# Banded convolution of a Conformer layer in eight time phases, its bands loaded from DRAM

## The chip, the cores and the metric

The kernel runs on one core of a Trainium2 chip. TensorE (PE) multiplies, VectorE (DVE), ScalarE (ACT) and GpSimd (POOL) work on elements, SyncE (SP) issues most of the DMAs; the engines run their own streams of instructions and meet only at semaphores. The metric is the device time of one launch in microseconds, lower is better.

## The reference

A decoder trunk of two layers on 512 tokens of 1024 channels, in float32: a Conformer convolution layer, then an attention layer, each followed by a mixture of experts. The change touches only the convolution of the first:

```python
def conformer_conv(h, w_in, b_in, w_dw, b_dw, ln_g, ln_b, w_out, b_out):
    u = h @ w_in + b_in
    a, gate = jnp.split(u, 2, axis=-1)
    u = a * jax.nn.sigmoid(gate)
    u = lax.conv_general_dilated(
        u, w_dw[:, None, :], window_strides=(1,), padding=[(CONV_KERNEL - 1, 0)],
        dimension_numbers=("NWC", "WIO", "NWC"), feature_group_count=D_MODEL) + b_dw
    u = jax.nn.silu(layer_norm(u, ln_g, ln_b))
    return u @ w_out + b_out
```

The convolution is depthwise and causal with 31 taps: each channel has its own filter over time.

## The kernel before

The 1024 channels are eight tiles of 128 partitions, with 512 time steps along the row. For each tile c the layer does this.

- `project_in(c)` on TensorE: 48 matmuls of 512 columns into two PSUM banks. A float32 operand is split into a leading part (`wih`, made by ScalarE's `leading_in`) and a trailing part (`wil`, VectorE's `trailing_in`), and three products are added. TensorE waits for `trailing_in(c)`, and for `gated(c - 2)`, which frees the banks.
- `sigmoid(c)` on ScalarE, `gated(c)` on VectorE: the gated product. ScalarE's stream is `leading_in(c)`, `sigmoid(c - 1)`, `leading_in(c + 1)` and so on; `leading_in(c)` waits until projection c - 2 is done.
- The convolution. Tiles 0, 2 and 4 (`BY_TAPS`) go over VectorE, 31 instructions each (`taps(c, first, last)`, then `tapped(c)`). Tiles 1, 3, 5, 6, 7 (`BY_BANDS`) go over TensorE in `convolve(c)`, with n = 0 to 4 as their place in that list.

For TensorE, time is cut in `PH` phases and the channels in `PH` blocks of `CB = 128 / PH`. The partitions then hold (phase, channel of one block), and for each block q a sum of `LAGS` matmuls with banded 128 x 128 weights `band[n % 2][:, q, m, :]` runs over `TP = 512 / PH` columns. A float32 matmul shows in the trace as two records. The tile gets into this form through DRAM: SP's `into_phases(c)` writes it to `u_dram` after `gated(c)`, waits, and reads it back in `PH` copies; `convolve(c)` waits for them. After it VectorE's `biased(c)` adds the bias into `yph`, and SP's `out_of_phases(c)` writes this to `c_dram`, waits, and reads it back into `HTQ` in `PH` copies.

The bands are built on VectorE by `spread(c)`: one product of 4608 elements per partition, of the taps with a diagonal of ones.

The mean over all channels (for the layer norm) is a matmul with 1/1024: VectorE adds up tiles 0 to 5 in `lnstd`, TensorE takes that sum, then tile 6 from `HTQ`, which waits for its way back from DRAM, and tile 7 straight from `yph[0]` in `PH` x `PH` matmuls with `onesp`. VectorE then subtracts the mean (`ln_d`), ScalarE squares, TensorE sums the squares, and the output projection follows.

Every engine's order is that of the code. SP's is one list of waits and copies: a step at its head that has to wait holds all that stand behind it. PE's order is projections 0, 1, 2, convolution 1, projections 3, 4, convolution 3, projections 5, 6, convolution 5, projection 7, convolutions 6 and 7.

Of the kernel before, what the change touches and what calls it, by code (L numbers as in the profile page):

```python
# [37 lines left out]
P = 128  # L38
D = 1024
# [19 lines left out]
PH = 4  # L59
CB = P // PH  # L60
TP = T // PH
# [26 lines left out]
C_BIN, C_BDW, C_LNG, C_LNB, C_ONE, C_TAP, C_WDW = 0, 16, 48, 56, 64, 96, 192  # L88
CONV_COLS = C_WDW + len(BY_BANDS) * PH * LAGS * PH

# [53 lines left out]
def build_program(nc, a):  # L144
# [7 lines left out]
    with ExitStack() as ctx:  # L152
# [95 lines left out]
        b_out_sb = cut(WR, 3 * 4096, D)  # L248
        WE = cut(WR, 52 * 256, 2, D)
# [4 lines left out]
        band = [at(f"band{b}", 108 + 18 * b, [P, PH, LAGS, P]) for b in range(2)]  # L254
# [18 lines left out]
        lnsq = [cut(SC, o + b * T, T) for b in range(2)]  # L273
        o += 2 * T
        onesf = cut(SC, o, P)
        o += P
        onesp = cut(SC, o, PH, P)
        o += PH * P
# [3 lines left out]
        o += T  # L282
        assert o <= 7680 - KT * (EG + E)
# [127 lines left out]
        wol_done, presum_done, band_set = [], [], []  # L411
# [83 lines left out]
        spread_set = Later(ln_n, KT + 1)  # L495
        spread_mm, spread_sb = Later(var_mm, KT), Later(sig_done, KT)
# [29 lines left out]
        def _(sp):  # L526
# [44 lines left out]
            into_phases(3)  # L571
            out_of_phases(1)
            win_load(7)
# [140 lines left out]
        def _(pool):  # L714
# [8 lines left out]
            nc.gpsimd.memset(onesp, 0.0).then_inc(conv_init, 1)  # L723
            pool.wait_ge(conv_init, 5)
            for r in range(PH):
                nc.gpsimd.memset(onesp[r * CB:(r + 1) * CB, r, :], 1.0 / D).then_inc(conv_init, 1)
                pool.wait_ge(conv_init, 6 + r)
# [113 lines left out]
        def _(act):  # L841
            act.dma_start(ident[:, :], a["ident"]).then_inc(const_in, 16)
            act.dma_start(vn[:, :], a["norm_vecs"]).then_inc(const_in, 16)
            act.dma_start(c16[:, :], a["c16"]).then_inc(const_in, 16)
            def norm_act(k):
# [48 lines left out]
            act.dma_start(b_out_sb[0:2 * CB, :], a["b_out"].to_broadcast([2 * CB, D])).then_inc(bout_in, 16)  # L894
# [27 lines left out]
            for h in range(2):  # L922
                nc.scalar.activation(bo[0:2 * CB, h * 512:(h + 1) * 512], b_out_sb[0:2 * CB, h * 512:(h + 1) * 512], ACT.Copy).then_inc(bout_added, 1)
            act.wait_ge(conv_init, 5 + PH)
            act.wait_ge(ug_out, 16 * len(BY_BANDS))
            nc.scalar.activation(bones[0:2 * CB, :], onesf[0:2 * CB, :], ACT.Copy, scale=float(D // CB)).then_inc(bout_added, 1)
# [265 lines left out]
        def _(dve):  # L1192
# [50 lines left out]
            def spread(c):  # L1243


                i, n = BY_BANDS.index(c), PH * LAGS * PH
                if i >= 2:
                    dve.wait_ge(conv_mm, i - 1)
                steps.mark(V.tensor_tensor(
                    band[i % 2][:, :, :, :].rearrange("p q m (r c) -> p (q m r) c", r=PH),  # L1250
                    cv[:, C_ONE:C_ONE + CB].rearrange("p (o c) -> p o c", o=1).to_broadcast([P, n, CB]),
                    cv[:, C_WDW + i * n:C_WDW + (i + 1) * n].rearrange("p (n o) -> p n o", o=1).to_broadcast([P, n, CB]),
                    ALU.mult))
                band_set.append(steps.n)

# [40 lines left out]
            spread(1)  # L1296
# [10 lines left out]
            spread(3)  # L1307
            taps(2, 0, 6)
            gated(3)
            biased(1)  # L1310
# [18 lines left out]
            spread(7)  # L1329
            taps(4, 14, 22)  # L1330
            gated(7)
# [1101 lines left out]
```

## Time and profile before

| | us |
|---|---|
| median of 3 runs | 1481.43 |
| lowest, highest | 1480.38, 1485.12 |
| the profiled execution, its time | 1482.62 |
| its span, first to last instruction | 1480.8 |
| the convolution layer's projections and convolutions in it | 16.5 to 146.1 |

The page of the profile gives busy times over the span; the timeline and the views by stretch show single stages; the chain of waits goes back from the last instruction, at each step to what released it. Rows of these views stand below in numbered groups.

### The profile page before, as it was taken

The numbers are of one execution on the slowest core, as the hardware profiler recorded it, in microseconds if no ns is written. First come the engines' busy times: TensorE is split into PE (matmuls) and PEld (weight loads), VectorE is DVE, ScalarE is ACT, GpSimd is POOL, SyncE is SP. The second block draws the span as 40 slices with busy tenths as digits, with TensorE's granted clock in tenths as the row PEclk, the third lists the DMA queues.
The fourth block names the chain that finished last, engine by engine and source line by source line (L and its number), as shares of the span: only waits on it lengthen the run. The fifth ranks groups of instructions, "written<-read, shape, count | busy, mean of one in ns | idle before, by whom it ended". The sixth has DMA issues, their size and how long they took to land.

```text
span 1480.8 us, 20665 instructions
## 1 busy us (share of the span) xinstructions
PE 1420.7 (96%) x7296; PEld 1156.7 (78%) x7296; DVE 1128.1 (76%) x1647; ACT 785.9 (53%) x1024; POOL 457.8 (31%) x330
## 2 busy tenths in 40 slices
PE   7999997999999997999999999999998899999997
PEld 5889685788888865888888888888887588888863
DVE  6999728888888869766858667585753888888866
ACT  5211835777777736344252533424353677777733
POOL 0000014344444410422405133150402544444310
PEclk9999997999999999999999999999999999999999
DMA  5242516899999954222212122131546599999872
GB/s 218 86 135 90 213 54 258 324 373 380 383 385 393 373 220 179 91 71 71 85 57 99 57 85 71 57 99 57 197 142 239 203 357 378 383 386 376 324 316 107
DMA packets 52765, 309.87 MB, mean 209 GB/s; under 512 B 10544, under 2 KB 16432, under 8 KB 38896
## 3 DMA queue, kind: packets, MB, share of 16 engines
q1 hardware_dynamic: 42128, 291.48, 51.3%
q0 software_dynamic: 9792, 16.80, 3.1%
q10 hardware_dynamic: 800, 1.00, 0.2%
q8 instruction: 27, 0.44, 0.1%
q14 instruction: 18, 0.15, 0.0%
HBM read 299.27 MB, written 28.84 MB: 222 GB/s over the span
## 4 chain that ended last, share of the span: by engine, by line
PE 87%; DVE 6%; DMA 2%; ACT 2%; issue 2%; POOL 0%; SPq 0%; DVEq 0%; POOLq 0%; ACTq 0%
PE PS L2185 5%; PE PS L2186 5%; PE PS L2187 5%; PE PS L2039 4%; PE PS L2038 4%; PE PS L2042 4%; PE PS L2025 4%; PE PS L2026 4%; PE PS L2027 4%; PE PS L2074 3%; PE PS L2075 3%; PE PS L2078 3%; PE PS L2201 3%; PE PS L2203 3%; PE PS L2202 3%; PE PS L2063 2%
## 5 line engine op out<-in xcount | busy, mean ns | idle before, releaser
L832 POOL TENSOR_TENSOR KQ<-rope_ab 64x512 f32<-64x512 f32 x96 | 173.6, 1809 | 316.5 <-DVE rope_ab L1698 312.9
L1573 DVE TENSOR_TENSOR wgl<-WR,wgh 128x2048 fp32r<-128x2048 f32 x66 | 150.9, 2293 | 39.3 <-ACT wgh L999 39.3
L1110 ACT ACTIVATE wh<-wraw 128x1024 fp32r<-128x1024 f32 x76 | 80.3, 1058 | 174.3 <-PE PS L2187 170.0
L1573 DVE TENSOR_TENSOR wul<-WR,wuh 128x2048 fp32r<-128x2048 f32 x66 | 148.4, 2288 | 5.2 <-issue 5.2
L1620 DVE TENSOR_TENSOR wdl<-WR,wdh 128x2048 fp32r<-128x2048 f32 x56 | 128.2, 2289 | 25.8 <-ACT wdh L1032 25.8
L1698 DVE TENSOR_TENSOR rope_ab<-PS,rope_sb 32x512 f32<-32x512 f32 x192 | 131.9, 687 | 2.6
L999 ACT ACTIVATE wuh<-WR 128x2048 fp32r<-128x2048 f32 x66 | 122.8, 1908 | 10.9 <-PE PS L2027 10.9
L1032 ACT ACTIVATE wdh<-WR 128x2048 fp32r<-128x2048 f32 x56 | 107.4, 1919 | 36.6 <-PE PS L2078 36.6
L999 ACT ACTIVATE wgh<-WR 128x2048 fp32r<-128x2048 f32 x66 | 125.1, 1903 | 0.0
L1680 DVE TENSOR_TENSOR wl<-wraw,wh 128x1024 fp32r<-128x1024 f32 x76 | 94.6, 1245 | 31.6 <-ACT wh L1110 30.1
L2038 PE MATMUL PS<-wgh,xgh 128*128 128x512 f32 x264 | 108.7, 412 | 1.4 <-ACT xgh L1015 1.4
L2039 PE MATMUL PS<-wgl,xgh 128*128 128x512 f32 x264 | 105.0, 398 | 0.0
L2025 PE MATMUL PS<-wuh,xgh 128*128 128x512 f32 x264 | 103.0, 390 | 0.0
L2027 PE MATMUL PS<-wuh,xgl 128*128 128x512 f32 x264 | 102.7, 389 | 0.0
L2026 PE MATMUL PS<-wul,xgh 128*128 128x512 f32 x264 | 102.7, 389 | 0.0
L769 POOL TENSOR_TENSOR idle<-ident_sb 128x1 f32<-128x1 f32 x30 | 20.8, 695 | 261.1 <-ACT SC L1053 248.9
L2074 PE MATMUL PS<-wdh,hTh 128*128 128x512 f32 x224 | 91.1, 407 | 0.0
L2075 PE MATMUL PS<-wdh,hTl 128*128 128x512 f32 x224 | 88.2, 394 | 0.0
L770 POOL DMA_INDIRECT y_dram<-SC,HTQ x30 | 79.4, 2646 | 5.3 <-issue 5.3
L2201 PE MATMUL PS<-HTh,wh 128*128 128x512 f32 x192 | 77.1, 402 | 0.0
L2203 PE MATMUL PS<-HTh,wl 128*128 128x512 f32 x192 | 74.9, 390 | 0.0
L2202 PE MATMUL PS<-HTl,wh 128*128 128x512 f32 x192 | 74.9, 390 | 0.0
(371 smaller groups left out, 3519.9 us busy)
## 6 DMA issues: line engine op xcount, KB each, us to landing
WR<-w_gate SPq DMA_DIRECT2D x33, 2048.0 KB, 12.0
WR<-w_up SPq DMA_DIRECT2D x33, 2048.0 KB, 9.3
WR<-w_down SPq DMA_DIRECT2D x33, 2048.0 KB, 12.0
wraw<-w_qkv SPq DMA_DIRECT2D x72, 512.0 KB, 3.3
WR<-w_in SPq DMA_DIRECT2D x8, 1024.0 KB, 4.9
xn_dram<-SC SPq DMA_DIRECT2D x8, 512.0 KB, 2.8
SC<-y_dram SPq DMA_DIRECT2D x8, 512.0 KB, 6.0
HT<-y_dram SPq DMA_DIRECT2D x8, 512.0 KB, 9.2
```

The lines of the kernel that those rows point to most:

```text
L832: nc.gpsimd.tensor_tensor(to, cos, sin, ALU.add).then_inc(rope_done, 1)
L999: nc.scalar.activation(dst[:, kts, :], src[:, kts, :], ACT.Copy).then_inc(done, 1)
L1573: V.tensor_tensor(lo[:, kts, :], raw[:, kts, :], hi[:, kts, :].bitcast(F32), ALU.subtract).then_inc(done, 1)
L1620: V.tensor_tensor(wdl[b][:, :, cols], wd[b][:, :, cols], wdh[:, :, :].bitcast(F32), ALU.subtract).then_inc(dl_done[l].sem, 1)
L1698: ins = V.tensor_tensor(rope_ab[d:d + 32, 2 * (t % 2) + 1, :], src[s:s + 32, :], rope_t[s:s + 32, tab + 1, :], ALU.mult)
L2025: M.matmul(dst, xgh[b][:, kt, :], hi[:, kt, :], start=kt == 0, stop=False)
L2026: M.matmul(dst, xgh[b][:, kt, :], lo[:, kt, :], start=False, stop=False)
L2027: ins = M.matmul(dst, xgl[b][:, kt, :], hi[:, kt, :], start=False, stop=kt == KT - 1)
L2038: M.matmul(PS[0][:, :], xgh[b][:, kt, :], wgh[:, kt, :], start=kt == 0, stop=False)
L2039: M.matmul(PS[0][:, :], xgh[b][:, kt, :], wgl[b][:, kt, :], start=False, stop=False)
L2074: M.matmul(to, hTh[:, ft, :], wdh[:, ft, :], start=ft == 0, stop=False)
L2075: M.matmul(to, hTl[:, ft, :], wdh[:, ft, :], start=False, stop=False)
```

## The change

`PH` becomes 8, so `CB` is 16, `TP` 64 and `LAGS` 5: a tile's convolution is 8 x 5 matmuls of 64 columns in place of 4 x 9 of 128, and each way into or out of phases reads back in 8 copies of 32 KB in place of 4 of 64 KB. The bands are laid out on the host, 20 KB per partition and tile, and ScalarE's queue loads them (`band_load`); `spread` and its constants are gone. The phases of tile 7 are summed by one VectorE reduction, so the mean takes 8 matmuls of 64 columns for them in place of 16 of 128. `b_out` is repeated over 32 rows as before, now named `BR`; `onesp` is one broadcast copy on GpSimd.

```diff
-PH = 4
+PH = 8
 CB = P // PH
+BR = 32
...
-        band = [at(f"band{b}", 108 + 18 * b, [P, PH, LAGS, P]) for b in range(2)]
+        band = [at(f"band{b}", 104 + 20 * b, [P, PH, LAGS, P]) for b in range(2)]
...
+        band_in = [Later(const_in, 48), Later(cvec_in, 16)]
...
             into_phases(3)
+            win_load(7)
             out_of_phases(1)
-            win_load(7)
             sp.dma_start(WE, a["w_out"][:, 0:2, :]).then_inc(wout_in[0], 16)
             out_of_phases(3)
...
+            def band_load(n):
+
+                if n >= 2:
+                    act.wait_ge(conv_mm, n - 1)
+                act.dma_start(band[n % 2].rearrange("p q m c -> p (q m c)"), a["bands"][n]).then_inc(band_in[n % 2].sem, 16)
...
             leading_in(1)
+            band_load(0)
             sigmoid(0)
             for c in range(2, KT):
                 leading_in(c)
                 sigmoid(c - 1)
+                if c % 2 == 0:
+                    band_load(c // 2)
+            band_load(4)
             sigmoid(KT - 1)
...
             trailing_in(4)
-            spread(3)
             taps(2, 0, 6)
             gated(3)
-            biased(1)
             taps(2, 6, 9)
...
             gated(4)
+            biased(1)
+            gated(5)
+            trailing_in(7)
             biased(3)
-            taps(4, 0, 3)
-            gated(5)
-            spread(5)
-            taps(4, 3, 4)
-            trailing_in(7)
-            spread(6)
-            taps(4, 4, 6)
+            taps(4, 0, 8)
             gated(6)
-            taps(4, 6, 14)
+            taps(4, 8, 14)
             biased(5)
-            spread(7)
-            taps(4, 14, 22)
+            taps(4, 14, 27)
             gated(7)
-            taps(4, 22, CONV)
+            taps(4, 27, CONV)
...
             biased(7)
+            dve.wait_ge(yph_done, len(BY_BANDS))
+            steps.mark(V.tensor_reduce(phase_sum, yph[0].rearrange("p (q t) -> p t q", q=PH), AX, ALU.add))
+            phases_summed.append(steps.n)
...
-                pe.wait_ge(v_steps, band_set[n])
+                pe.wait_ge(band_in[n % 2].sem, band_in[n % 2].at(16 * (n // 2 + 1)))
...
-            pe.wait_ge(yph_done, len(BY_BANDS))
+            pe.wait_ge(v_steps, phases_summed[0])
             for r in range(PH):
-                for q in range(PH):
-                    ins = M.matmul(PS[4][:, r * TP:(r + 1) * TP], onesp[:, r, :], yph[0][:, q * TP:(q + 1) * TP],
-                                   start=False, stop=r == PH - 1 and q == PH - 1)
+                ins = M.matmul(PS[4][:, r * TP:(r + 1) * TP], onesp[:, r, :], phase_sum, start=False, stop=r == PH - 1)
```

How the order moves is seen at two places. The first is VectorE between the last step of tile 2's taps and `gated(6)`; L1265 is `gated`, L1290 `biased`, L1249 `spread`, `wil` is written by `trailing_in`, L1273 to L1278 are taps. Before:

```order
L1282 TENSOR_TENSOR HTQ<-taps_sb 128x512 [waits v_steps]
L1265 SCALAR_TENSOR_TENSOR taps_sb<-PS,SC 128x4x128 [waits sig_done,taps_done]
L1290 TENSOR_TENSOR SC<-PS,SC 128x512 [waits conv_mm]
L1273 TENSOR_SCALAR taps_sb<-taps_sb,SC 128x512 [waits glu_done]
L1275 TENSOR_SCALAR taps_sb<-taps_sb,SC 128x512
L1278 SCALAR_TENSOR_TENSOR taps_sb<-taps_sb,SC 128x512 [waits v_steps]
L1265 SCALAR_TENSOR_TENSOR SC<-PS,SC 128x512 [waits ug_out,sig_done]
L1249 TENSOR_TENSOR band_115<-SC 128x4608 [waits conv_mm]
L1278 SCALAR_TENSOR_TENSOR taps_sb<-taps_sb,SC 128x512 [waits v_steps]
L1237 TENSOR_TENSOR wil_122<-WR,wih_120 128x2048 [waits lead_done]
```

And now, with `trailing_in` at L1250:

```order
L1282 TENSOR_TENSOR HTQ<-taps_sb 128x512 [waits v_steps]
L1265 SCALAR_TENSOR_TENSOR taps_sb<-PS,SC 128x8x64 [waits sig_done,taps_done]
L1290 TENSOR_TENSOR SC<-PS,SC 128x512 [waits conv_mm]
L1265 SCALAR_TENSOR_TENSOR SC<-PS,SC 128x512 [waits ug_out,sig_done]
L1250 TENSOR_TENSOR wil_122<-WR,wih_120 128x2048 [waits lead_done]
L1290 TENSOR_TENSOR SC<-PS,SC 128x512 [waits conv_mm]
L1273 TENSOR_SCALAR taps_sb<-taps_sb,SC 128x512 [waits glu_done]
L1275 TENSOR_SCALAR taps_sb<-taps_sb,SC 128x512
L1278 SCALAR_TENSOR_TENSOR taps_sb<-taps_sb,SC 128x512 [waits v_steps] x6
L1265 SCALAR_TENSOR_TENSOR SC<-PS,SC 128x512 [waits ug_out,sig_done]
```

The first L1290 of the old rows is `biased(3)`, right behind `gated(4)`; in the new rows the first is `biased(1)`, and `biased(3)` is the second, behind `gated(5)` and `trailing_in(7)`.

The second place is SP's queue from the way into phases of tile 3 to that of tile 5. Before (L546, L553 into phases, L559, L563 out of them, L540 a load of `w_in`, L574 and L576 loads of `w_out`):

```order
L559 DMA c_dram<-SC 128x512 [waits yph_done]
L563 DMA HTQ<-c_dram 32x4x128 [waits yph_out]
L563 DMA HTQ<-c_dram 32x4x128 x3
L540 DMA WR<-w_in 128x2048 [waits wil_done]
L574 DMA WR<-w_out 128x2x1024
L559 DMA c_dram<-SC 128x512 [waits yph_done]
L563 DMA HTQ<-c_dram 32x4x128 [waits yph_out]
L563 DMA HTQ<-c_dram 32x4x128 x3
L576 DMA WO<-w_out 128x2x1024
L546 DMA u_dram<-SC 128x512 [waits glu_done]
L553 DMA SC<-u_dram 32x4x128 [waits conv_mm,conv_init,ug_out]
L553 DMA SC<-u_dram 32x4x128 x3
```

And now:

```order
L546 DMA WR<-w_in 128x2048 [waits wil_done]
L565 DMA c_dram<-SC 128x512 [waits yph_done]
L569 DMA HTQ<-c_dram 16x8x64 [waits yph_out]
L569 DMA HTQ<-c_dram 16x8x64 x7
L580 DMA WR<-w_out 128x2x1024
L565 DMA c_dram<-SC 128x512 [waits yph_done]
L569 DMA HTQ<-c_dram 16x8x64 [waits yph_out]
L569 DMA HTQ<-c_dram 16x8x64 x7
L582 DMA WO<-w_out 128x2x1024
L552 DMA u_dram<-SC 128x512 [waits glu_done]
L559 DMA SC<-u_dram 16x8x64 [waits conv_mm,conv_init,ug_out]
L559 DMA SC<-u_dram 16x8x64 x7
```

The load of `w_in` for projection 7 moved ahead of tile 1's way out; the ways out of tiles 1 and 3 still stand ahead of the way in of tile 5, each with twice the copies.

## Rows read from the trace of the kernel before

**Rows 1.** The page, busy time of each engine over the span.

```profile
PE 1420.7 (96%) x7296; PEld 1156.7 (78%) x7296; DVE 1128.1 (76%) x1647; ACT 785.9 (53%) x1024; POOL 457.8 (31%) x330
```

**Rows 2.** TensorE by stretch: us, busy (records), granted clock, DMA share, GB/s.

```profile
99.10:110.00 10.90, 10.90 (x49) 1.00 0.53 164
110.00:118.90 8.90, 8.20 (x74) 1.00 0.13 44
```

**Rows 3.** Chain of waits, 93 to 120 us: start, us, what.

```profile
96.53 2.94 DMA c_dram<-SC
...
101.29 0.43 SPq L576
...
101.77 5.68 DMA u_dram<-SC
...
108.76 1.97 DMA SC<-u_dram
...
110.78 8.30 PE PS L1946 x72
```

**Rows 4.** Chain of waits, 0 to 260 us, TensorE's runs of records.

```profile
130.01 16.08 PE PS L1946 x144
146.09 0.86 PE PS L1967 x2
...
147.81 3.58 PE PS L1973 x32
...
205.31 1.70 PE PS L1835 x16
```

**Rows 5.** Groups by line and shape, 0 to 240 us: busy us, mean ns.

```profile
L1249 DVE TENSOR_TENSOR band<-SC 128x4608 f32<-128x4608 f32 x5 | 24.8, 4951 | 0.0
...
L1835 PE MATMUL PS<-SC,XT 128*128 128x20 f32 x64 | 8.4, 277 | 0.8 <-DVE XT L1384 0.8
```

**Rows 6.** The page, DMA issues: count, KB each, median us to landing.

```profile
WR<-w_up SPq DMA_DIRECT2D x33, 2048.0 KB, 9.3
...
WR<-w_in SPq DMA_DIRECT2D x8, 1024.0 KB, 4.9
```

**Rows 7.** DMA issues, 0 to 200 us: count, KB each, median us to landing.

```profile
u_dram<-SC SPq DMA_DIRECT2D x5, 256.0 KB, 2.0
SC<-u_dram SPq DMA_DIRECT2D x20, 64.0 KB, 2.0
```

**Rows 8.** Timeline of SP's queue, 0 to 165 us: start, us of issuing, copies.

```profile
43.13 1.75 SPq L553 DMA_DIRECT2D SC<-u_dram  x4
...
72.93 1.76 SPq L553 DMA_DIRECT2D SC<-u_dram  x4
...
135.84 0.43 SPq L582 DMA_DIRECT2D WO<-w_out  x1
139.87 0.34 SPq L559 DMA_DIRECT2D c_dram<-SC  x1
142.78 1.74 SPq L563 DMA_DIRECT2D HTQ<-c_dram  x4
```

**Rows 9.** Timeline, 95 to 111 us, VectorE and ScalarE: start, us, instruction.

```profile
95.83 0.67 DVE L1290 TENSOR_TENSOR SC<-PS,SC 128x512 f32<-128x512 f32 x1
...
99.23 0.69 ACT L903 ACTIVATE SC<-PS,SC 128x512 f32<-128x512 f32 x1 [16.45 <-PE PS L1935]
...
99.82 1.91 ACT L891 ACTIVATE wih<-WR 128x2048 fp32r<-128x2048 f32 x1
...
106.15 2.29 DVE L1237 TENSOR_TENSOR wil<-WR,wih 128x2048 fp32r<-128x2048 f32 x1
```

**Rows 10.** TensorE by stretch around an idle time, columns as in the second group.

```profile
164.70:167.40 2.70, 2.67 (x6) 0.50 1.10 464
167.80:170.50 2.70, 2.70 (x14) 1.00 0.74 309
```

**Rows 11.** VectorE's groups by line and shape: a reduction.

```profile
L1538 DVE TENSOR_REDUCE HTQ<-HTQ 128x8 f32<-128x384 f32 x2 | 1.1, 555 | 0.1
```

More of the change, by code:

```diff
@@ L87 @@
                  ((0, 0, 0), (0, 1, 0), (0, 1, 1), (0, 2, 0)), ((0, 2, 1), (0, 3, 0), (0, 3, 1)))
-C_BIN, C_BDW, C_LNG, C_LNB, C_ONE, C_TAP, C_WDW = 0, 16, 48, 56, 64, 96, 192
-CONV_COLS = C_WDW + len(BY_BANDS) * PH * LAGS * PH
+C_BIN, C_BDW, C_LNG, C_LNB, C_SEL, C_TAP = 0, 16, 80, 88, 96, 104
+CONV_COLS = C_TAP + len(BY_TAPS) * (CONV + 1)
 class Steps:
@@ L273, in build_program @@
         lnsq = [cut(SC, o + b * T, T) for b in range(2)]
+        onesp = cut(SC, o, PH, P)
+        assert PH * P <= 2 * T
         o += 2 * T
@@ L276, in build_program @@
         o += P
-        onesp = cut(SC, o, PH, P)
-        o += PH * P
+        b_out_sb = cut(SC, o, D)
+        o += D
         cv = cut(SC, o, CONV_COLS)
@@ L282, in build_program @@
         o += T
+        phase_sum = cut(SC, o, TP)
+        o += TP
         assert o <= 7680 - KT * (EG + E)
@@ L410, in build_program @@
         fin_g = cut(WR, 4096, D)
-        wol_done, presum_done, band_set = [], [], []
+        wol_done, presum_done, phases_summed = [], [], []
         beats = {(l, stage): [] for l in range(2) for stage in ("rank", "rows")}
@@ L722, in _ @@
                 nc.gpsimd.memset(uph[b][:, :, 0:LAGS - 1], 0.0).then_inc(conv_init, 1)
[L723 to L727, printed above, removed]
+            pool.wait_ge(cvec_in, 16)
+            nc.gpsimd.tensor_copy(onesp, cv[:, C_SEL:C_SEL + PH].rearrange("p (r o) -> p r o", o=1).to_broadcast([P, PH, P])).then_inc(conv_init, 1)
             def moe_pool(l):
@@ L922, in _ @@
             for h in range(2):
[L923 to L924 removed]
+                nc.scalar.activation(bo[0:2 * BR, h * 512:(h + 1) * 512], b_out_sb[0:2 * BR, h * 512:(h + 1) * 512], ACT.Copy).then_inc(bout_added, 1)
+            act.wait_ge(conv_init, 4)
             act.wait_ge(ug_out, 16 * len(BY_BANDS))
[L926 removed]
+            nc.scalar.activation(bones[0:2 * BR, :], onesf[0:2 * BR, :], ACT.Copy, scale=float(D // BR)).then_inc(bout_added, 1)
             act.wait_ge(conv_mm, len(BY_BANDS))
@@ L1242, in _ @@
             dve.wait_ge(cvec_in, 16)
[L1243 to L1254, printed above, removed]
             def gated(c):
@@ L1844, in project_out @@
                         for h in range(2):
-                            M.matmul(PS[2 * n + h][:, :], bones[0:2 * CB, :], bo[0:2 * CB, h * 512:(h + 1) * 512], start=True, stop=False)
+                            M.matmul(PS[2 * n + h][:, :], bones[0:2 * BR, :], bo[0:2 * BR, h * 512:(h + 1) * 512], start=True, stop=False)
                     for n in range(NT):
@@ L1962, in _ @@
             convolve(7)
-            pe.wait_ge(conv_init, 4)
-            pe.wait_ge(conv_init, 9)
+            pe.wait_ge(conv_init, 5)
             pe.wait_ge(v_steps, presum_done[0])
@@ L2397, in lay_out @@
     by_block = np.tile(f["a_b_dw"][0].reshape(KT * PH, CB).T, (PH, 1))
-    same = np.tile(np.eye(CB, dtype=np.float32), (PH, 1))
+    of_phase = (np.arange(P)[:, None] // CB == np.arange(PH)).astype(np.float32) / np.float32(D)
+    taps_of = np.zeros((len(BY_BANDS), PH, CB, PH, LAGS, PH, CB), np.float32)
+    for c in range(CB):
+        taps_of[:, :, c, :, :, :, c] = bands[:, c][:, list(BY_BANDS)].transpose(1, 0, 2, 3, 4)
     a = {"x": f["x"]}
@@ L2402, in lay_out @@
     a["ffn_norm"] = f["ffn_norm"].reshape(2, 1, D)
-    a["conv_vecs"] = asc(cat([by_tile(f["a_b_in"][0]), by_block, by_tile(f["a_ln_g"][0]), by_tile(f["a_ln_b"][0]), same, taps,
-                              bands[:, :, list(BY_BANDS)].reshape(P, -1)], 1))
+    a["conv_vecs"] = asc(cat([by_tile(f["a_b_in"][0]), by_block, by_tile(f["a_ln_g"][0]), by_tile(f["a_ln_b"][0]), of_phase, taps], 1))
+    a["bands"] = taps_of.reshape(len(BY_BANDS), P, PH * LAGS * P)
     a["w_in"] = asc(f["a_w_in"][0].reshape(P, KT, 2, KT, P).transpose(3, 0, 1, 2, 4).reshape(KT, P, KT * 2 * P))
```

8 lines of the change are left out of this document (3 added, 5 removed).

## The prediction

> **What bounds the kernel now.** The page comes first: TensorE (PE) is busy 96% of the span [rows 1]. Next come the busy times by stretch: over the projections and convolutions of layer 0 TensorE is full, and the one gap is 0.7 us before the convolution of tile 5 [rows 2]. The reader is to see that there VectorE's work, long as it is, already hides under TensorE. Third, the chain of waits up to that gap shows what the slack hangs on [rows 3]: VectorE's `biased(3)` ends at 96.5, SP writes tile 3 to `c_dram` (2.94 us), issues its reads, one 1 MB load of `w_out`, then the write of tile 5 to `u_dram` (5.68 us, since the megabyte is ahead of it in the same queue), then the reads of tile 5, and `convolve(5)` starts at 110.78. From the end of `biased(3)` to that matmul are 14.25 us, and they fit only because `biased(3)` comes 2.6 us before TensorE ends projection 5 (about 99.1).
>
> **The change part by part.** All numbers are on the clock of the trace of before until the sum.
>
> *Convolution on TensorE.* A tile was 4 x 9 matmuls of 128 columns and is now 8 x 5 of 64. A matmul in float32 shows as two records, so 72 records become 80. Now 144 records take 16.08 us, 111.7 ns each [rows 4]. Do 64 columns cost half? The router's matmuls stream 20 columns against weights of 128 columns, also float32 [rows 5], and 16 of them take 1.70 us, 106.3 ns each [rows 4]. With a sixth of the columns the record is hardly shorter: the weight load sets it. So 64 columns cost between 106.3 and 111.7 ns; I take 106.3, as the fewer columns lie below the load. 80 x 106.3 ns = 8.50 us against 8.04, so +0.46 a tile, +2.3 us for five (4.5 at the upper price). All of it is on the path, as TensorE is full. The Trainium skill (TensorE: Matmul & The Clock Gate, section LDWEIGHTS) says that a weight load costs by its columns, P / 1.2 ns, 107 ns for 128, whatever streams afterwards; it speaks against the halving, and by it the five tiles come to +2.6 us, while by the same page's section Back-to-back issue gap, whose isolated gap counts the moving columns alone, they would shrink; the 20-column row agrees with the first.
>
> *Bands from DRAM.* Five VectorE instructions, 24.8 us in all, go [rows 5]. They hide under TensorE today, so this gives nothing by itself: `gated(1)`, `gated(3)`, `gated(5)` and `trailing_in(6)` wait for ScalarE's steps, which wait for TensorE. Instead ScalarE issues five loads of 2.5 MB. 1 MB lands in 4.9 us and 2 MB in 9.3 [rows 6]; 2.5 MB in some 9 to 12. Every band is asked for 10 us or more before its convolution (the last right after `convolve(5)`, 19 us before `convolve(7)`), so no band is late. But bands 1 and 2 are issued just as SP sends tiles 1 and 3 through DRAM. See below.
>
> *Small copies.* Each way back from DRAM is eight issues instead of four, some 0.48 us apart (four take 1.75 us, each lands 2.0 after its issue) [rows 7, 8], so the last piece is 1.9 us later. Before, tile 1's four reads were issued from 43.13 on and had landed at about 46.6, for a convolution at 50.3: slack 3.7. With 1.9 more it is 1.8. Tile 3 has its reads from 72.93 and the convolution at 80.1: slack 3.7, then 1.8. The band load beside each takes some of it; the write and the reads may each be a microsecond or two slower. I take 0.5 us of wait at each, +1.0 together (0 to 10, see the second rival). Pieces are 256 B instead of 512 B. The Trainium skill (DMA: Bandwidth & Descriptors, Specifications) puts the least size for full rate at 512 B, which no row here tests; at 32 KB a copy I leave the term as it is.
>
> *The reordering, the main term.* `biased(3)` stood right after `gated(4)`. Now `biased(1)`, `gated(5)` and `trailing_in(7)` are ahead of it, and both of these wait for the end of projection 5. ScalarE: the sigmoid starts at 99.23, the next step at 99.82 [rows 9]. Between them now lies one DMA issue, say 0.45, so the leading part runs 100.3 to 102.2, `trailing_in(7)` takes 2.25 and `biased(3)` 0.6 [rows 9]: it ends at about 105.0 instead of 96.5. SP's order has not followed: `out_of_phases(3)` is still ahead of `into_phases(5)`. The chain of 14.25 us starts at 105.0 and is longer by two sets of four issues, 3.8 us: 18.1, ending at 123.1. There is more ahead of its first write: `out_of_phases(1)` is now late too (`biased(1)` ends about 96.5, eight reads until 102.5), so the 1 MB load WE goes out at about 103 rather than 79.8, and band load 3 (2.5 MB, issued about 100) is in flight; a write behind 1 MB took 5.68 [rows 3] against a median of 2.0 [rows 7]. I take +2 (0 to 4.5): `convolve(5)` can start at 125.1, and TensorE is ready at 109.9. It waits 15.2 us instead of 0.9, +14.3. If the write of tile 5 were not held by the megabyte ahead of it (2.0 for 5.68) and the first write not at all, +8.6; at the other end +16.8. Queued behind the wait are projection 7 and convolutions 6 and 7; VectorE stands at `biased(5)` and ScalarE at band load 4 meanwhile.
>
> *Clock.* After the idle stretch up to 164.7 TensorE has a granted clock of 0.50, the 1.2 GHz level, for 2.7 us and 1.00 after it [rows 10]. A wait of 15 us should end so as well: some 3.4 us at half pace, +1.7 (0 to 2).
>
> *Tile 7.* `gated(7)` ends about 1.9 us after projection 7; write 2.0, last issue 3.4, landing 2.0: 9.3 us after the projection's end, while convolution 6 takes 8.5. +0.8 (0 to 2).
>
> *The mean.* 32 records of 3.58 us [rows 4] become 16, 1.7 us at 106.3: -1.9. VectorE's reduction reads 512 elements (384 took 0.56 [rows 11]), 0.6 to 1.1 us, and lies with `biased(7)` beside the two matmuls of 1.72 us before it. Given back: the second of these waits for tile 6 from DRAM. Its write sits behind the load of `w_out` that TensorE's last projection releases; one such write took from 139.87 to 142.78 with that load 4 us ahead [rows 8], now it is 1.6 ahead, and eight issues follow. That lands 10.1 us after `convolve(6)`, against 9.4 for `convolve(7)` and the first matmul: +0.7. Net -1.2. The late `w_out` load of `out_of_phases(7)` arrives about when ScalarE wants it.
>
> **Sum.** 2.3 + 1.0 + 14.3 + 1.7 + 0.8 - 1.2 = 18.9. Later stages follow in the same order, shifted. The profiled execution took 1482.6 with a span of 1480.8; 1482.6 + 18.9 = 1501.5. It lay 1.2 above the median of the three runs, so between 1500.3 and 1501.5: I say 1501.
>
> **Rivals.** *A, the forecast:* `convolve(5)` starved through `biased(3)`, 1501.
>
> *B, the small copies are held at every band load.* If the write and reads of tiles 1 and 3 get through only once the band is in (9 to 12 us after its issue at 40.3 and 70.1, then 5.4 for reads), those convolutions wait 4.5 to 7 us each: 1501.5 - 1.0 + 9 to 14 = 1510 to 1515. For: the 5.68 us write. Against: that one stood behind a load in its own queue, and the bands come from another. The Trainium skill (DMA: Bandwidth & Descriptors, Queues, rings and completion order) has each DMA engine go round its queues by packets, which would keep the small copies moving; no row here shows two queues at once.
>
> *C, not slower: the columns set the price.* Two records of 512 columns take 0.86 us [rows 4], 0.84 ns a column; 64 would be 54 ns and a tile 4.3 us, 3.7 less than before. Five tiles: -18.7 in place of +2.3; tile 7 then waits about 5.0 instead of 0.8; the mean saves 0.8 more: 1501.5 - 21.0 + 4.2 - 0.8 = 1484, no change, and with the short end of the wait (5.7 less) 1478, faster. It decides from a record of some 60 ns on. Against: the 20-column row at 106 ns.
>
> *D, no change: the chain is not late.* If tile 5 were there by 109.9, 14.3, 1.7 and 0.9 go: about 1484. Against: its start hangs on the end of projection 5 through two engines, and even the shortest copies need over 10 us from there.
>
> **How the numbers follow.** A 0.78, B 0.13, C 0.05, D 0.04. A measurement of this kernel tells about 0.3%, 4.4 us, from no change. A and B are slower, so is a part of D; C is mostly the same, a part faster: slower 0.93, same 0.05, faster 0.02. The low end takes the short chain and free copies at tiles 1 and 3 with a little back: 1501 - 5.7 - 1 - 2.5 = 1492. The high end takes half of B: 1511.
>
> **What would show it.** In the profile after: `convolve(5)` starts 10 us or more after projection 6 ends, released by a DMA into SC; the chain of waits runs from ScalarE's leading part through `trailing_in(7)`, `biased(3)`, both `c_dram` and `u_dram` writes; `biased(5)` shows a long idle time ahead of it; convolution records come at 106 to 112 ns; the clock reads 0.50 early in `convolve(5)`; the mean's matmuls take 1.7 us. I am wrong if `convolve(5)` starts on time, if the records come near 55 ns, or if the waits at tiles 1 and 3 are larger than the one at tile 5.

## The result, and the profile after

The changed kernel takes 1551.09 us (median of 4 runs, 1547.19 to 1552.36), the kernel before 1482.39 (4 runs, 1480.38 to 1485.12). The ratio is 1.0458 (95% interval 1.0432 to 1.0484), slower by 69 us. The forecast was 1501, with a range from 1492 to 1511: the sign was right, the size was not. The profiled execution took 1552.36 us with a span of 1550.5.

The page, busy time of each engine over the span, answers to [rows 1]:

```profile
PE 1464.3 (94%) x7320; PEld 1196.2 (77%) x7320; DVE 1105.7 (71%) x1643; ACT 787.1 (51%) x1024; POOL 458.9 (30%) x326
```

TensorE has *more* busy time and a smaller share, so it both waits and works more slowly. Where it does so is seen in TensorE by stretch (columns as in [rows 2]: stretch, us, busy and records, granted clock, DMA share, GB/s). The stretches are projection 1; the wait for tile 1, its convolution, the projection after it; the same for tile 3; the same for tile 5; convolution 6; the wait for tile 7 and its convolution:

```profile
39.00:49.80 10.80, 10.80 (x49) 1.00 0.72 267
49.80:55.10 5.30, 0.10 (x1) 0.88 0.32 62
55.20:72.50 17.30, 17.30 (x81) 0.50 0.31 119
72.50:84.30 11.80, 11.80 (x50) 0.92 0.00 0
...
95.00:100.30 5.30, 0.29 (x3) 0.80 0.36 70
100.30:117.60 17.30, 17.30 (x81) 0.50 0.23 82
117.60:131.00 13.40, 13.40 (x51) 0.83 0.25 84
...
141.60:157.00 15.40, 0.04 (x1) 0.64 0.45 131
157.00:174.40 17.40, 17.36 (x81) 0.50 0.08 21
174.40:186.40 12.00, 12.00 (x50) 0.90 0.64 244
186.40:195.30 8.90, 8.90 (x81) 1.00 0.29 77
195.30:196.90 1.60, 0.07 (x1) 1.00 0.62 94
196.90:214.10 17.20, 17.16 (x81) 0.51 0.28 88
```

Read the clock column first. The four convolutions that follow a wait of TensorE run at 0.50, the 1.2 GHz level, to their last record, three of them from the first on and that of tile 7 but for its first records: 17.1 to 17.3 us. The one that follows a projection without a gap runs at 1.00 in 8.9. In the kernel before every convolution took 8.04 to 8.3 [rows 3, 4].

From the start to the end of the last convolution the shift is 214.1 - 146.1 = 68.0 us:

| part | before | after | difference |
|---|---|---|---|
| waits ahead of tiles 1, 3, 5, 7 | 0.7 | 5.3 + 5.0 + 15.4 + 1.6 = 27.3 | +26.6 |
| convolutions 1, 3, 5, 7 | 3 x 8.04 + 8.30 = 32.4 | 3 x 17.33 + 17.13 = 69.1 | +36.7 |
| convolution 6 | 8.0 | 8.9 | +0.9 |
| the projections behind 1, 3 and 5 | 3 x 10.8 | 11.8 + 13.4 + 12.0 | +4.8 |

The wait at tile 3 is 5.0 us, since the first 0.29 of its stretch still belongs to the projection. The sum is 69.0. TensorE is ready for tile 1 half a microsecond sooner than before, and with that the parts close on 68.0 to within half a microsecond. Behind the convolutions the spans differ by (1550.5 - 214.1) - (1480.8 - 146.1) = 1.7 us: the 16 records at the head of the output projection take 9.3 us at a mean clock of 0.82, from 220.9 on, where they took 7.7 at 1.00. So nearly all is decided in the first 230 us.

What ends the waits stands in the chain of waits of the changed kernel (start, us, what), cut to the copies through DRAM and what is around them. It answers to [rows 3] (SC holds the tile on its way through DRAM):

```profile
40.57 9.51 DMA u_dram<-SC
...
53.30 1.85 DMA SC<-u_dram
55.19 17.33 PE PS L1942 x80
...
85.94 8.98 DMA u_dram<-SC
...
98.14 2.10 DMA SC<-u_dram
100.29 17.33 PE PS L1942 x80
...
131.39 1.91 ACT wih L900
133.32 2.29 DVE wil L1250
135.61 0.61 DVE SC L1290
136.24 5.92 DMA c_dram<-SC
...
146.34 5.56 DMA u_dram<-SC
...
157.04 17.34 PE PS L1942 x80
...
175.12 9.72 DMA c_dram<-SC
...
196.94 17.13 PE PS L1942 x80
214.07 1.81 PE PS L1962 x2
215.88 1.71 PE PS L1964 x2
217.59 1.85 PE PS L1967 x16
```

Two things are to be seen. The chain to tile 5 (131.39 to 157.04) is the one that the prediction drew: leading part, `trailing_in(7)`, `biased(3)`, both writes, eight reads. And the writes of tiles 1 and 3, for which the prediction had 2.0 us and at most a microsecond or two more, took 9.51 and 8.98. From the end of a write to the landing of the last read it is 5.1 to 5.3 us at tiles 1, 3 and 5, as foreseen for eight issues. The DMA issues of 0 to 230 us (count, KB each, median us to landing) answer to [rows 7]:

```profile
band<-bands ACTq DMA_DIRECT2D x5, 2560.0 KB, 10.8
u_dram<-SC SPq DMA_DIRECT2D x5, 256.0 KB, 5.6
...
SC<-u_dram SPq DMA_DIRECT2D x40, 32.0 KB, 1.9
```

The reads in pieces of 256 B land as fast as those of 512 B did (1.9 against 2.0). The median of the five writes to `u_dram` rose from 2.0 to 5.6 us. ScalarE's timeline shows when the band beside the first of those writes is sent:

```profile
39.07 0.33 ACTq L852 DMA_DIRECT2D band<-bands  x1
```

This band load takes 10.75 us and lands at 49.8; the write in SP's queue goes out at 40.57 and lands at 50.1. The other loads go out at 84.44, 130.80 and 174.40, and the first writes behind them, of 85.94, 136.24 and 175.12, land at 94.9, 142.2 and 184.8. The four writes thus land 11.0, 10.5, 11.4 and 10.4 us after the issue of the band, though they were issued 0.7 to 5.4 us behind it; the four bands land at 49.8, 94.7, 141.6 and 184.6, each 0.2 to 0.6 us ahead of its write. A write lands when the band is in, not sooner. The DMA queues' records by stretch (queue, records, MB, share of the 16 engines) show how, first from 40.5 to 44.5 us, then from 44.5 to 50.2; q10 is ScalarE's queue with the band, q1 SP's with the write:

```profile
q10 hardware_dynamic: 64, 1.31, 79.8%
q1 hardware_dynamic: 1, 0.00, 0.1%
```

```profile
q10 hardware_dynamic: 66, 1.02, 45.8%
q1 hardware_dynamic: 143, 0.26, 11.9%
```

In the first four microseconds after the write's issue the engines take 64 records of the band and one of the write's 144. After that the two queues go side by side (from 44.5 to 47.0 us 45 records of the band and 38 of the write), and the write's last records go behind those of the band.

### The profile page after: what moved, and what is told of

Same layout as the page of the kernel before. It is cut to its first block, busy times and chain, and to the rows that moved or that the text cites. A ratio compares the mean times of both kernels' runs of the same rounds, so it can differ in the third digit from the quotient of the medians.

```text
span 1550.5 us, 20749 instructions
## 1 busy us (share of the span) xinstructions
PE 1464.3 (94%) x7320; PEld 1196.2 (77%) x7320; DVE 1105.7 (71%) x1643; ACT 787.1 (51%) x1024; POOL 458.9 (30%) x326
## 4 chain that ended last, share of the span: by engine, by line
PE 85%; DVE 5%; DMA 4%; ACT 2%; issue 2%; SPq 1%; ACTq 0%; DVEq 0%; POOLq 0%
PE PS L2178 5%; PE PS L2179 5%; PE PS L2180 5%; PE PS L1942 4%; PE PS L2031 4%; PE PS L2032 4%; PE PS L2035 4%; PE PS L2018 3%; PE PS L2020 3%; PE PS L2019 3%; PE PS L2067 3%; PE PS L2068 3%; PE PS L2071 3%; PE PS L2194 3%; PE PS L2196 3%; PE PS L2195 3%
## 5 line engine op out<-in xcount | busy, mean ns | idle before, releaser
L1012 ACT ACTIVATE wuh<-WR 128x2048 fp32r<-128x2048 f32 x66 | 122.8, 1910 | 10.8 <-PE PS L2020 10.8
L1942 PE MATMUL PS<-SC,band 128*128 128x64 f32 x400 | 78.2, 392 | 27.3 <-DMA SC<-u_dram 27.3
L1942 PEld LDWEIGHTS PS<-SC,band 128*128 128x128 f32 x400 | 77.5, 304 | 28.7 <-DMA SC<-u_dram 28.7
L772 POOL TENSOR_TENSOR idle<-ident_sb 128x1 f32<-128x1 f32 x30 | 20.8, 695 | 261.1 <-ACT SC L1066 248.7
L912 ACT ACTIVATE SC<-PS,SC 128x512 f32<-128x512 f32 x8 | 5.5, 689 | 149.3 <-PE PS L1931 142.7
## 6 DMA issues: line engine op xcount, KB each, us to landing
band<-bands ACTq DMA_DIRECT2D x5, 2560.0 KB, 10.8
```

Of the source, the lines that this page charges most:

```text
L1012: nc.scalar.activation(dst[:, kts, :], src[:, kts, :], ACT.Copy).then_inc(done, 1)
L1942: ins = M.matmul(PS[6 + n % 2][:, q * TP:(q + 1) * TP], band[n % 2][:, q, m, :], uph[n % 2][:, q, LAGS - 1 - m:LAGS - 1 - m + TP], start=m ...
```

## The experiments

The theory after this result has three parts. *Held writes:* a write waits for the band load that another queue has issued just ahead of it. *Late bias:* the order of VectorE's steps makes tile 5 late. *Cold stream:* a convolution of 64-column records that TensorE enters after a wait stays at the low clock until it ends. Against the first stands that the writes are slow through their own shape, that of eight phases. Against the third stands that the 64-column convolution is slow for another reason: beside DMA traffic, or by what it reads.

### The bands issued apart from the writes

```diff
             band_load(0)
+            band_load(1)
             sigmoid(0)
...
                 leading_in(c)
+                if c in (4, 6):
+                    band_load(c // 2)
                 sigmoid(c - 1)
-                if c % 2 == 0:
-                    band_load(c // 2)
```

Band 1 goes out behind band 0, bands 2 and 3 one step of ScalarE sooner.

> The changed kernel (1551) with its band loads moved away from the small copies: band 1 is issued right behind band 0, band 2 ahead of sigmoid(3), band 3 ahead of sigmoid(5). Theory (small copies are held while a band is loading, the convolution then starts after an idle time at the 1.2 GHz level, and 80 records of 64 columns never bring the clock back): the two waits of 5.3 us go, the convolutions of tiles 1 and 3 take about 9 instead of 17.3 us, the projections behind them lose no more time, and the first write of the chain to tile 5 is no longer held: about 1516. Rival 1 (the convolutions are slow for themselves, whatever the clock): only the waits go, 1536 to 1540. Rival 2 (the 256-byte pieces hold the copies, not the bands): no change, 1551.

Measured: 1528.02 us (1519.53 to 1528.9), ratio 1.0291 (1.0258 to 1.0325). The DMA issues of 0 to 230 us:

```profile
u_dram<-SC SPq DMA_DIRECT2D x5, 256.0 KB, 2.0
```

The writes of tiles 1 and 3 take 2.0 us again in the same shape: it is not the shape, it is the band beside it. (That of tile 5 takes 5.63 behind a 1 MB load of its own queue, and tile 5's way out, 0.7 us behind the last band, still 9.73.) Tile 3 no longer waits and its convolution takes 8.9 us at 1.00. The wait at tile 1 is down to 1.06 us. It has another cause: the two bands at the start of the layer hold the load of `w_in`, for which ScalarE's leading part of tile 2 waits 3.22 us, and so the write of tile 1 goes out at 43.32 instead of 40.57. And yet, after this one microsecond, the clock falls inside the convolution and stays down to its end (TensorE by stretch, the convolution from its start on):

```profile
50.40:53.00 2.60, 2.56 (x22) 0.95 0.39 91
53.00:56.00 3.00, 3.00 (x16) 0.50 0.66 276
56.00:65.50 9.50, 9.50 (x47) 0.50 0.11 30
```

So I had expected 1516 and got 1528: a wait of one microsecond costs the clock too. At tile 5 a wait of 12.97 us is left, its convolution all at 0.50 (17.3 us); at tile 7 there is one of 0.76, and the clock falls inside the convolution as at tile 1 (15.1 us).

### VectorE's and SP's order put back

```diff
             gated(3)
+            biased(1)
             taps(2, 6, 9)
...
             gated(4)
-            biased(1)
+            biased(3)
             gated(5)
             trailing_in(7)
-            biased(3)
...
-            win_load(7)
             out_of_phases(1)
+            win_load(7)
```

> The changed kernel (1551) with biased(1) behind gated(3), biased(3) behind gated(4) and SP's win_load(7) behind out_of_phases(1), as in the kernel before; band loads as changed. Theory: biased(3) runs as soon as convolution 3 ends, some 18 us after that tile 5 is there, before projection 6 ends; the wait of 15.4 us at tile 5 goes and its convolution takes 9 instead of 17.3 us, the waits at tiles 1 and 3 stay: about 1526. Rival 1 (convolutions slow for themselves): 1536. Rival (the wait at tile 5 is not from the order): no change.

Measured: 1541.9 us (1539.21 to 1541.93), ratio 1.0402 (1.0384 to 1.0419), far less of a gain than expected. The waits are 4.04 at tile 1, 5.04 at tile 3 and 5.18 at tile 5, all three convolutions at 0.50 again, but for the first records of tile 1. Order alone does not empty the wait at tile 5. The chain of waits to it no longer goes through `biased(3)`, whose write takes 2.05 us and is done long before:

```profile
131.36 9.31 DMA u_dram<-SC
...
143.88 1.95 DMA SC<-u_dram
```

Band load 3 goes out at 129.86, 1.5 us ahead of this write, and tile 5 now waits for the same reason as tiles 1 and 3, a wait that the late `biased(3)` had hidden. So the order was worth the 10.2 us of waiting that went, and with neither edit alone does the clock come back at tile 5.

> Both edits together on the changed kernel. Theory: no wait at tiles 1 and 3; at tile 5 the chain of 18.1 us starts near 97.5 and ends near 115.6 while projection 6 ends near 112, so a wait of some 4 us stays and with it a convolution at the low clock (17.3 us), the same at tile 7 with its short wait: about 1508. If every convolution but the last keeps the full clock, 1496. Rival 1 (convolutions slow for themselves): five at 17 us, 1528 or more.

With both edits: 1508.06 us (1504.87 to 1511.02), ratio 1.0172 (1.0151 to 1.0194), as expected. TensorE by stretch: convolution 1 after a wait of 0.54 us; then the start of convolution 7, after a wait of 0.77, and its rest:

```profile
51.00:60.00 9.00, 8.99 (x81) 1.00 0.33 118
...
155.60:158.00 2.40, 2.37 (x19) 0.87 0.88 316
...
161.00:171.00 10.00, 10.00 (x49) 0.50 0.12 26
```

After 0.54 us without work the clock stays up for all 80 records; after 0.77 it falls within the first 20 or so and does not come back before the convolution's end. The length of the wait need not be what decides between the two: the one stands behind a projection, the other behind convolution 6, itself 80 records of 64 columns, and no run separates these. The wait at tile 5, 3.36 us, had nearly the whole convolution at 0.50 (17.1 us).

### TensorE given unused work in its waits

To tell a cold stream (one that runs at the 1.2 GHz level) from one that is slow by itself, the waits are kept and only the idleness goes: ahead of convolutions 1, 3, 5, 6 and 7, and of their wait for data, TensorE issues 32, 32, 93, 0 and 10 bf16 matmuls whose results nobody reads.

```diff
                 n = BY_BANDS.index(c)
+                for _ in range((32, 32, 93, 0, 10)[n]):
+                    M.matmul(PS[4][:, 0:3 * P], ident_b, c16b[:, 0:3 * P], start=True, stop=True)
                 pe.wait_ge(uph_in[n % 2], (n // 2 + 1) * PH * 16)
```

> The changed kernel (1551) with matmuls into an unused PSUM bank ahead of the convolutions of tiles 1, 3, 5 and 7 (32, 32, 93 and 10 of 384 columns in bfloat16), sized to fill their waits; their results are not used. Nothing else is changed, so all waits for copies stay. Theory: the clock stays at 1.00 through the waits, each of the four convolutions takes about 9 instead of 17.3 us and the projections behind lose nothing: 1551 - 33 - 4 = 1513. Rival 1 (not the clock, but short columns or traffic make the records 217 ns long): 1551 or a little more.

Measured: 1516.44 us (1514.25 to 1523.67), ratio 1.0225 (1.0206 to 1.0244): 35 us given back by work that is of no use (28.7 between the profiled executions, 1552.36 and 1523.67, of which 3 x 8.3 are convolutions 1, 3 and 5). TensorE by stretch, the convolution of tile 1 (that of tile 5 reads alike, from 137.7 to 146.7), then a part of that of tile 7, ahead of which ten fillers left a wait of 2.12 us:

```profile
55.60:64.60 9.00, 9.00 (x83) 1.00 0.53 192
...
175.00:187.00 12.00, 12.00 (x57) 0.50 0.10 23
```

Same records, same data, with DMA traffic up to 192 GB/s beside them: what differs is the granted clock, and they take 9.0 us instead of 17.3. So the stream is not slow by itself, it is cold. These stretches also give the price of a record at full clock: 9.0 us for 80, 112.5 ns, as good as the 111.7 of a 128-column record [rows 4].

The Trainium skill (TensorE: Matmul & The Clock Gate, What's actually happening) says that the array speeds up after sustained work and falls back when it goes idle. In the changed kernel the fall agrees (a mean of 0.88 over the wait at tile 1, 0.64 over that at tile 5); the rise does not: in [rows 10] it came after 2.7 us, in each of the convolutions 1, 3 and 5 TensorE is busy for 17.3 us without a gap in the records, and the clock does not rise.

### Four phases: is it the width of the records?

The kernel before is made to wait ahead of convolution 1, with its 128-column records:

```diff
                 sp.wait_ge(ug_out, 16 * (n + 1))
+                if n == 0:
+                    sp.wait_ge(wil_done, 5)
```

> The kernel before (1482) with one wait added: SP reads tile 1 back only after trailing_in(4), so that convolution 1, 72 records of 128 columns, is entered after an idle time of some 14 us. Theory: its first 3 to 4 us are at the 1.2 GHz level, then 1.00 again; it takes 10 us instead of 8: 1482 + 14 + 2 = 1498. Rival (weight-bound streams stay at the low clock, whatever the columns): 16.1 us, 1505.

Measured: 1498.27 us (1496.89 to 1499.45), ratio 1.0112 (1.0095 to 1.0129). TensorE stands for 13.9 us; then comes the convolution, in two stretches:

```profile
64.40:68.00 3.60, 3.60 (x17) 0.50 0.97 389
68.00:74.60 6.60, 6.60 (x58) 0.95 0.24 98
```

With 128 columns the clock is back after some 4 us and the convolution takes 10.2 us, 2 more than at full clock. This is the price that the prediction had put in (+1.7); it holds for the old record and not for the new one.

The converse is the changed kernel, bands, order and mean as they are, with four phases in place of eight:

```diff
-PH = 8
+PH = 4
```

(the columns of the small constants in `conv_vecs` move with it).

> The changed kernel (1551) with PH = 4 and nothing else: bands still loaded from DRAM beside the copies, VectorE's new order and the new mean stay; a convolution is 72 records of 128 columns again. Theory (the low clock lasts through a whole convolution because of its 64-column stream): the waits stay but for four issues a way, 3.4 us each at tiles 1 and 3 and 11 to 12 at tile 5, while the 128-column stream comes back to 1.00 after some 3 us as other stages do, so each convolution entered after a wait takes 10 instead of 17.3 us: 1482 + 19 + 6 - 1 = 1506. Rival (any stream with a weight load for each matmul stays at the low clock): three convolutions at 16 us, 1524 or more.

Measured: 1499.2 us (1494.07 to 1500.7), ratio 1.011 (1.0088 to 1.0131). The waits are 2.15, 2.10 and 10.54 us. Convolution 5, entered cold:

```profile
126.70:130.00 3.30, 3.30 (x15) 0.50 0.29 84
130.00:133.80 3.80, 3.80 (x24) 0.64 0.04 10
133.80:138.00 4.20, 4.20 (x39) 1.00 0.02 4
```

It recovers within the convolution. Convolution 1 keeps 1.00 throughout after its wait of 2.15 us, and that of tile 3, after 2.10, is at 0.83 in the mean and takes 9.9: after waits twice as long as the one that cost the 64-column stream its clock, the first loses nothing here and the second 2 us. (The writes of tiles 1 and 3, beside their bands, take 8.17 and 8.06 us here: held writes belong to the bands, not to eight phases.) Of the 69 us, 52 go with the eight phases alone, that is with the narrower record and with eight copies in place of four: the cold convolutions themselves, the copies (1.9 us a tile), and the later steps that these push apart. How large this share is depends on the rest of the kernel, as the last experiments show.

### The old kernel with the new order

```diff
             gated(3)
-            biased(1)
...
             gated(4)
-            biased(3)
-            taps(4, 0, 3)
+            biased(1)
             gated(5)
-            spread(5)
-            taps(4, 3, 4)
             trailing_in(7)
+            biased(3)
+            spread(5)
             spread(6)
-            taps(4, 4, 6)
+            taps(4, 0, 6)
...
-            out_of_phases(1)
             win_load(7)
+            out_of_phases(1)
```

> The kernel before (1482) with VectorE's biased(1) and biased(3) moved behind gated(4) and behind trailing_in(7), and win_load(7) ahead of out_of_phases(1), as in the changed kernel; four phases and bands built by VectorE. Theory: the chain of 14.25 us to tile 5 starts near 104.5 instead of 96.5 and has the load of w_out ahead of its first write, convolution 5 waits 9 to 12 us and takes 2 more: 1482 + 11 + 2 = 1495. Rival (the wait at tile 5 comes from the eight copies and the band loads, not from the order): 1482 to 1486.

Measured: 1492.16 us (1490.82 to 1493.38), ratio 1.0072 (1.0055 to 1.0088). The wait at tile 5 is 8.63 us. Its chain of waits, at the end of `biased(3)`, has the write that answers to the first of [rows 3]:

```profile
104.83 2.71 DMA c_dram<-SC
```

`biased(3)` ends at 104.8 where it was 96.5; the prediction said 105.0. The reordering alone costs 10 us. The wait in the changed kernel is longer by its eight issues per tile and by the write of tile 3, which took 5.92 us for 2.71.

### Eight phases with everything else mended

Bands apart, order back, and fillers of 8, 0, 24, 0, 8 (first run) or 22 at the end (second run):

> Eight phases with everything against the waits: bands apart from the copies, biased(1) and biased(3) back, and 8, 24 and 8 matmuls into an unused bank ahead of the convolutions of tiles 1, 5 and 7 to hold the clock. Theory: all five convolutions near 9.0 us at a clock of 1.00 (80 records of 112 ns), which is 1 us each more than before; waits and fillers of 7 us; the shorter mean gives 1.7 back: 1482 + 5 + 7 - 2 = 1492. Rival (64-column records have the price of half the columns at the full clock): 1470.

Measured: 1499.9 us (1493.8 to 1501.27), ratio 1.0117 (1.009 to 1.0144). Eight fillers were too few: tile 7 still waited 1.51 us, the clock fell 1.4 us into its convolution, and it took 16.0 us.

> As eight_kept_warm (1500), with 22 in place of 8 unused matmuls ahead of the convolution of tile 7, whose wait of 1.5 us had let the clock fall. Theory: all five convolutions now run at 1.00 and take 9.0 us; the last goes from 16 to 9, the filler costs no more than a microsecond: 1493. It gives the price of eight phases with the clock held: about 1 us a tile over four phases. Rival (the last convolution is slow for another reason, the traffic of the last loads): 1500.

Measured: 1494.74 us (1491.14 to 1495.72), ratio 1.0077 (1.0059 to 1.0094). All five convolutions run at 1.00, in 9.0 us each.

So even with the order of before, free writes and the full clock, eight phases stay 12 us behind: 9.0 us a tile for 8.04 is 4.8 of them; by the end of convolution 7 it is 12.4 (158.5 for 146.1), the other 7.6 being the later tiles, whose waits the fillers now fill, and the fillers themselves, which no run separates. What the shorter mean then saves, the output projection gives back, its first 16 records again taking 9.3 us for 7.7 at a clock of 0.82.

### What the other parts are worth

All but the eight phases, with bands apart and order back, leaves the DRAM bands and the new mean:

> The changed kernel with PH = 4, its band loads apart from the small copies and biased(1), biased(3) and win_load(7) back in place: what is left of the change is bands from DRAM and the new mean. Theory (VectorE's 24.8 us of band building was hidden, so its removal gives nothing; only the mean pays): 1479 to 1482. Rival (VectorE's freed time does reach the end): 1475 or less. If band traffic still holds a copy: 1484 or more.

Measured: 1480.4 us (1477.5 to 1482.77, 11 runs) against 1481.75 (21 runs), ratio 0.9991 (0.9982 to 1.0): nothing that can be told from no change. The 24.8 us taken off VectorE [rows 5] give no time: the gain is smaller than that of the new mean by itself, next. Tile 5 waits 1.58 us here, for 0.70 before, and the output projection starts at 150.92, as with the new mean alone (150.81). This kernel and that with both edits (1508.06) differ in `PH` alone: with the bands apart and the order put back, eight phases cost 28 us, where they cost 52 with both as changed.

The new mean alone, in the kernel before:

```diff
             biased(7)
+            dve.wait_ge(yph_done, len(BY_BANDS))
+            steps.mark(V.tensor_reduce(phase_sum, yph[0].rearrange("p (q t) -> p t q", q=PH), AX, ALU.add))
...
-            for r in range(PH):
-                for q in range(PH):
-                    ins = M.matmul(PS[4][:, r * TP:(r + 1) * TP], onesp[:, r, :], yph[0][:, q * TP:(q + 1) * TP],
+            for r in range(PH):
+                ins = M.matmul(PS[4][:, r * TP:(r + 1) * TP], onesp[:, r, :], phase_sum, start=False, stop=r == PH - 1)
```

> The kernel before (1481.8) with the new mean alone, four phases: VectorE sums the phases of tile 7, the matmuls for it are 4 in place of 16. Theory: 32 records of 3.6 us become 8 of 0.9, the reduction lies beside the two matmuls ahead but for some 0.3 us: -2.4, 1479.4. With the moved load of before_new_mean (1477.7, both edits) the rest of 1 to 1.7 us is the wait at tile 5. Rival (the gain is given back in the layer norm): 1481 to 1482.

Measured: 1479.0 us (1477.35 to 1480.64, 11 runs) against 1482.47 (15 runs), ratio 0.998 (0.9971 to 0.9989). Last, the same with the load of `WO[:, 6:8]` moved behind `into_phases(5)`:

> The kernel before (1482.4) with two edits: the four phases of tile 7 summed by VectorE ahead of the mean, and SP's load of w_out for tiles 6 and 7 moved behind the way into phases of tile 5. Theory: the mean's matmuls for tile 7 take 0.9 instead of 3.6 us, less some 0.3 us of waiting for the reduction, and the wait of 0.9 us at tile 5 goes: 1479 to 1480. Rival (the layer norm then waits for tile 7 from DRAM or for the weights): 1482.

Measured: 1477.72 us (1477.12 to 1480.13, 11 runs) against 1481.75 (21 runs), ratio 0.9974 (0.9965 to 0.9983). It is 4.0 us ahead of the kernel before and has the lowest median here, though its interval overlaps that of the mean alone. The gap ahead of convolution 5 is gone. The chain of waits of both kernels, that of the mean alone first, tells what holds the output projection then:

```profile
146.32 3.90 ACT WOh L920 x4
...
150.81 7.72 PE PS L1981 x16
```

```profile
144.74 3.90 ACT WOh L920 x4
...
149.23 7.72 PE PS L1981 x16
```

In place of the mean's records it is ScalarE's four leading parts of `w_out` (L920), which it begins when convolution 7 ends. The output projection starts at 152.82 in the kernel before, at 150.81 with the new mean, at 149.23 with both.

## Why the prediction was right in sign and wrong in size

**Clock, the step that failed.** The prediction took from [rows 10] that the low level lasts 2.7 us, and wrote "a wait of 15 us should end so as well: some 3.4 us at half pace, +1.7". Those rows are of 512-column matmuls. Entered cold, the stream of 64-column records stayed at 0.50 for all 17.3 us, four times: +36.7 us in place of +1.7 and the record's price, and +4.8 in the projections behind. (Its 3.4 us is a little more than the 2.7 of the rows.) It also charged the clock for tile 5 alone and gave the 0.8 us at tile 7 none, though the runs lost 6 to 7 us of convolution after waits of 0.59 to 1.06 us. I carried a row over to another kind of work without naming that as a choice; a bound "the whole convolution at half pace" would have been 8 us for one wait and 33 for the four that came.

**Waits at tiles 1 and 3.** Predicted +1.0 together (0 to 10), measured 10.3. Rival B had the mechanism and its first price (4.5 to 7 us each) and was given 0.13. The argument against it was that the one slow write in the rows stood behind a load of its own queue. The runs show that a load of another queue does the same: 9.0 to 9.7 us beside a band, 2.0 in the same kernel with the band sent at another time. The queue records show the load's records going first, 64 against 1 in the first four microseconds. The prediction had cited the Trainium skill (DMA: Bandwidth & Descriptors, Queues, rings and completion order) for small copies going on between the packets of a load. The same section gives a packet as some 9 to 17 descriptors. The whole band is 144 records, 9 for each of 16 engines: by that figure one turn is about the whole load, so the rule, counted out, stood with rival B, and I had cited it without the count. This trace agrees in part. The engines do stay with the band at first, but not for the whole of it: by its share a band record takes 0.80 us (4 us x 16 x 0.798 / 64), the eight large ones of an engine 6.4, and the write's first record goes about 4.4 us after the band's first. Why the write still lands only behind the band is not shown. Rival B's total, 1510 to 1515, was too low, since it had no clock for the waits at tiles 1 and 3.

**Wait at tile 5.** Predicted 15.2 us, measured 15.4, by the chain as drawn. From the end of projection 5 to that of `biased(3)` it was 5.4 us (5.9 forecast), from there to the convolution 20.8 (20.1): the first write was slower than forecast, 5.92 us for 4.9, the step before it and the copies a little faster, and that these small misses cancel to 0.2 us is luck. The order alone, at four phases, gave a wait of 8.63 and cost 10 us.

**Records.** Half the columns did not make a shorter record, as forecast, against rival C. But of the two bounds the upper one was right: 112.5 ns (9.0 us for 80) and not 106.3, so +0.9 to +1.0 us a tile where +0.46 was taken. At the low clock, in four of the five convolutions, a record took 214 to 217 ns, which neither bound had.

**Tile 7.** Predicted +0.8, measured 1.6, plus a convolution at half pace for it.

**The mean.** 16 records took 1.85 us for 3.58, -1.7 where -1.9 was forecast, and the wait for tile 6 (+0.7) did not come. But the two pairs of matmuls ahead (L1962, L1964) ran at the low clock, 1.81 and 1.71 us for 0.86 each [rows 4], which took it back. At full clock, in the kernel before with its four phases, the new mean is worth 3.5 us. The output projection starts 2.0 us sooner; another 0.8 lies at 237 to 242 us of the profiled execution, where eight records take 1.15 us at a clock of 1.00 and took 1.97 at 0.50 before. The rest was not traced.

**VectorE's bands.** Hidden before, no gain now: right.

**Readings and sums.** The wait at tile 5 before is 0.7 us [rows 2], not the 0.9 that was taken off, and `trailing_in(7)` takes 2.29 [rows 9], not 2.25; both are small. The upper end of the range, "half of B: 1511", does not follow from B: half of its 9 to 14 us on 1500.5 gives 1505 to 1507.5. The measured 1551 is far above either.

**What would show it.** Larger waits at tiles 1 and 3 than at tile 5 did not come. A clock of 0.50 early in `convolve(5)` did, and it did not end; the records at 106 to 112 ns came, near 112, in convolution 6 alone. The sign that the text lacked was a convolution at 0.50 to its last record.

## What to carry to other kernels

Before a stream is cut into narrower matmuls, ask what happens to it when it starts cold: here a convolution entered at the low clock lost 2 to 3 us with 128 columns and 8 with 64, and waits of 0.6 to 1.1 us ahead of the narrow stream cost 6 to 7, where one of 0.7 ahead of the wide one had cost nothing. A large load on one queue and a small copy on another are not independent when the copy is on the path: send the load where nobody waits for small copies. And when an order is changed on one engine, the steps of the queue that carries its results (here SP's) must be moved with it.

## What the runs showed of the hardware

- A stream of float32 matmuls of 64 columns entered at the 1.2 GHz level stayed there for 17.3 us with TensorE busy throughout (changed kernel, tiles 1, 3 and 5); one of 128 columns was at 2.4 GHz again after some 4 to 6 us (3.6 us at 0.50 and then a mean of 0.95 in the kernel before when held; 3.3 at 0.50 and 3.8 at 0.64 in the changed kernel with four phases). With unused bf16 matmuls in the wait the 64-column stream took 9.0 us at 1.00.
- After a wait of 0.54 us the granted clock stayed at 1.00 through 80 such records; after 0.59, 0.76, 0.77 and 1.06 us (0.59 with the order put back, tile 7) it fell to 0.50 some 1.8 to 2.4 us into the stream and stayed there to its end. Waits of 0.70 us (kernel before, tile 5 [rows 2]) and 2.15 us (changed kernel with four phases, tile 1) ahead of 128-column records left it at 1.00; after 2.10 us (there, tile 3) it was 0.83 in the mean.
- In the changed kernel a write of 256 KB took 9.0 to 9.7 us when it was issued 0.7 to 1.5 us behind a 2.5 MB load of the other queue and 5.9 us when issued 5.4 behind it, and 2.0 us without it; it landed 0.2 to 0.6 us after the load did. Copies of 32 KB in pieces of 256 B landed in 1.9 us, as before in 2.0 with pieces of 512 B.
- At the full clock a float32 record took nearly the same for 64 and for 128 columns: 112.5 ns (unused work in the waits, tile 1) and 111.7 (kernel before [rows 4]).
